# Last token group of an encoder layer: residual copied to the output, scaled tiles added to it by stores of GpSimd

## The reference, cut to what matters

```python
u = rms_norm(h, norm_pre)
p = u @ w_in                      # attention and linear-attention inputs, gates
y_a = (attention(...) * silu(za)) @ w_branch_attn
y_g = (rms_norm(gla(...)) * silu(zg)) @ w_branch_gla
merged = sigmoid(ga + b) * y_a + sigmoid(gg + b) * y_g
h = h + rms_norm(merged @ w_out, norm_post)
```

## Time and profile before

| | us |
|---|---|
| median of 3 runs | 2850.39 |
| lowest, highest | 2848.67, 2850.72 |
| profiled execution, whole time | 2849.08 |
| its span, first to last instruction | 2847.3 |
| TensorE busy in the span | 2746.1 |
| VectorE busy | 2120.7 |
| ScalarE busy | 1205.7 |
| GpSimd busy | 78.7 |
| DMA, mean rate | 160 GB/s |

### The profile page before, as it was taken

One profiled execution on the slowest core, in us unless ns is written; L12 is line 12 of the kernel. 1 busy time (PEld: TensorE's weight loads), 2 busy tenths in 40 slices (PEclk: granted clock), 3 DMA queues, 4 the chain that ended last, 5 costly groups with the idle time before them and its releaser, 6 DMA issues. The chain is left out here.

```text
span 2847.3 us, 52025 instructions
## 1 busy us (share of the span) xinstructions
PE 2746.1 (96%) x20860; PEld 2603.7 (91%) x20860; DVE 2120.7 (74%) x3375; ACT 1205.7 (42%) x1972; POOL 78.7 (3%) x55
## 2 busy tenths in 40 slices
PE   7999999998999999999999999999899999999996
PEld 7999999998999999999777887878799999999996
DVE  7898777778787787777777777787576877655556
ACT  5343333445354333344555566565422322442331
POOL 0221000000000000000000000000000000000001
PEclk9999999999999999999999999999999999999998
DMA  4555333345344333344656565565534555555664
GB/s 152 164 185 177 122 128 127 122 132 209 100 141 142 123 128 128 120 133 133 193 164 187 171 190 177 165 191 167 194 133 170 212 198 198 170 173 184 184 195 138
DMA packets 234186, 456.95 MB, mean 160 GB/s; under 512 B 23904, under 2 KB 139744, under 8 KB 233072
## 3 DMA queue, kind: packets, MB, share of 16 engines
q1 hardware_dynamic: 233968, 453.91, 49.8%
HBM read 365.90 MB, written 88.47 MB: 160 GB/s over the span
## 5 line engine op out<-in xcount | busy, mean ns | idle before, releaser
L2164 PE MATMUL bank<-th,w_hi 128*128 128x272 f32 x2360 | 687.3, 291 | 8.7 <-DVE w_lo L1429 6.4
L2164 PE MATMUL bank<-tl,w_hi 128*128 128x272 f32 x2360 | 682.7, 289 | 0.0
L2164 PE MATMUL bank<-th,w_lo 128*128 128x272 f32 x2360 | 682.0, 289 | 0.0
L2164 PEld LDWEIGHTS bank<-th,w_hi 128*128 128x128 f32 x2360 | 445.2, 189 | 13.1 <-DVE w_lo L1429 8.0
L1416 DVE TENSOR_TENSOR w_lo<-w_raw,w_hi 128x1024 fp32r<-128x1024 f32 x224 | 273.8, 1223 | 239.2 <-ACT w_hi L989 238.8
L1004 ACT ACTIVATE w_hi<-w_more 128x1024 fp32r<-128x1024 f32 x236 | 250.3, 1061 | 469.7 <-DVE w_more L1448 247.8
L2164 PEld LDWEIGHTS bank<-tl,w_hi 128*128 128x128 f32 x2360 | 445.3, 189 | 1.0 <-issue 1.0
L2164 PEld LDWEIGHTS bank<-th,w_lo 128*128 128x128 f32 x2360 | 444.9, 189 | 0.0
L989 ACT ACTIVATE w_hi<-w_raw 128x1024 fp32r<-128x1024 f32 x224 | 236.8, 1057 | 365.9 <-PE bank L2476 228.0
L1429 DVE TENSOR_TENSOR w_lo<-w_more,w_hi 128x1024 fp32r<-128x1024 f32 x236 | 295.1, 1251 | 111.0 <-ACT w_hi L1004 108.8
L2142 PE MATMUL bank<-uh,w_hi 128*128 128x272 f32 x1024 | 317.0, 310 | 13.5 <-DVE w_lo L1416 8.6
(11 more groups left out here) (278 smaller groups left out, 5653.1 us busy)
## 6 DMA issues: line engine op xcount, KB each, us to landing
w_raw<-in_w_tiles SPq DMA_DIRECT2D x344, 512.0 KB, 4.1
w_more<-in_w_tiles SPq DMA_DIRECT2D x120, 512.0 KB, 3.6
p_scratch<-stage SPq DMA_DIRECT2D x44, 544.0 KB, 3.0
gl<-p_scratch SPq DMA_DIRECT2D x24, 512.0 KB, 5.7
w_pair<-in_w_tiles SPq DMA_DIRECT2D x9, 1024.0 KB, 8.7
gate_scratch<-stage SPq DMA_DIRECT2D x16, 544.0 KB, 3.0
gate_scratch<-stage SPq DMA_DIRECT2D x64, 136.0 KB, 4.2
gate_even<-gate_scratch SPq DMA_DIRECT2D x8, 1088.0 KB, 6.8
```

Source lines behind the costliest of these rows:

```text
L2164: ins = pe.matmul(out[:, 0:GAW], wt[:, k], ut[:, k], start=start and k == 0 and i == 0, stop=stop and k == HK - 1 and i == 2, skip_group_c ...
```

## The change

The residual of the last group is no longer loaded into `x_last`. In place of the first `load_last`, behind the first pair of group 1, SyncE issues one transfer that copies all 2048 rows of the last group's tokens from `xT` to `yT`, from DRAM to DRAM. The wait for the products of group 0 that stood ahead of the first load is gone, and so are the other three loads. In the tail VectorE only scales; its additions and those of GpSimd are gone. GpSimd waits for the copy, and then for each pair of scaled tiles, and issues a store of the pair with an accumulating operation: what is stored is added to what lies in `yT`. SyncE no longer issues the last stores and only waits for them.

```diff
--- before.py
+++ after.py
@@ -489,10 +489,9 @@
         s_sld = sem("state_loaded")
 
         s_g = [sem("gates_of_even_pairs_loaded"), sem("gates_of_odd_pairs_loaded")]
-        s_xl = sem("last_residual_loaded")
+        s_xl = sem("last_residual_copied")
         s_yl = sem("last_output_stored")
         s_sc2 = sem("last_output_scaled")
-        s_add = [sem("last_even_tiles_added"), sem("last_odd_tiles_added")]
         s_oev2 = sem("output_tiles_evacuated")
         s_ssz = sem("square_sums_cleared")
         s_sqo = sem("output_squares_summed")
@@ -955,24 +954,13 @@
                         next_w(PASS_OUT + g * KT + m, m)
                         store_y(g - 1, n, m, r)
 
-                def load_last(k):
-
-                    a, w = GRP[2]
-                    sp.dma_start(x_last[:, k:k + 4, 0:w], x_view[:, k:k + 4, a:a + w]).then_inc(s_xl, 16)
-
                 pair(0)
                 if g == 1:
-                    sp.wait_ge(s_mo, 2 * KT)
-                load_last(8 * (g - 1))
+                    a, w = GRP[2]
+                    sp.dma_start(yT[:, a:a + w], xT[:, a:a + w]).then_inc(s_xl, 16)
                 with sp.Fori(1, KT // 2 - 1) as i:
                     pair(i)
-                load_last(8 * (g - 1) + 4)
                 pair(KT // 2 - 1)
-            a, w = GRP[2]
-            for i in range(KT // 2):
-                for r in range(2):
-                    sp.wait_ge(s_add[r], i + 1)
-                sp.dma_start(yT.rearrange("(k p) t -> p k t", p=P)[:, 2 * i:2 * i + 2, a:a + w], out_sb[2][:, 2 * i:2 * i + 2, 0:w]).then_inc(s_yl, 16)
             sp.wait_ge(s_yl, 16 * KT // 2)
             sp.wait_ge(s_kv, 16 * 6)
             sp.wait_ge(s_sst, 32)
@@ -1401,12 +1389,12 @@
                 gla_roots(it, DEC if it == N_IT - 1 else P)
             for n in range(3):
                 roots(n + 2, 3)
-            w = GRP[2][1]
-            for k in range(1, KT, 2):
-                pool.wait_ge(s_sc2, k + 1)
-                if k == 1:
-                    pool.wait_ge(s_xl, 16 * KT // 4)
-                pool.tensor_tensor(out_sb[2][:, k, 0:w], out_sb[2][:, k, 0:w], x_last[:, k, 0:w], ALU.add).then_inc(s_add[1], 1)
+            a, w = GRP[2]
+            y_view = yT.rearrange("(k p) t -> p k t", p=P)
+            pool.wait_ge(s_xl, 16)
+            for k in range(0, KT, 2):
+                pool.wait_ge(s_sc2, k + 2)
+                pool.dma_start(y_view[:, k:k + 2, a:a + w], out_sb[2][:, k:k + 2, 0:w], accum_op=ALU.add).then_inc(s_yl, 16)
 
 
         @block.vector
@@ -2126,11 +2114,6 @@
             for k in range(KT):
                 dve.scalar_tensor_tensor(out=out_sb[2][:, k, 0:w], in0=out_sb[2][:, k, 0:w], scalar=norm_sb[:, 1, k:k + 1],
                                          in1=rso[:, 0:w], op0=ALU.mult, op1=ALU.mult).then_inc(s_sc2, 1)
-                if k % 2 == 0:
-                    dve.wait_ge(s_sc2, k + 1)
-                    if k == 0:
-                        dve.wait_ge(s_xl, 16 * KT // 4)
-                    dve.tensor_tensor(out_sb[2][:, k, 0:w], out_sb[2][:, k, 0:w], x_last[:, k, 0:w], ALU.add).then_inc(s_add[0], 1)
 
 
         @block.tensor
```

## The result

The changed kernel took 2859.93 us in the median of 7 runs (2856.66 to 2861.8), the kernel before 2848.67 us in the 7 runs beside them (2846.24 to 2850.72). The ratio is 1.0035, with a 95% interval of 1.0025 to 1.0045: slower by about 10 us, 0.35% (the two medians lie 11.3 us apart). The profiled execution's span grew from 2847.3 to 2858.2 us, by 10.9 us.

A forecast was written before the change was run, and what follows sets the result against it. TensorE, busy for 96% of the span, was taken to bound the kernel, another engine only behind its last product. Stall 7.1, clock 2.0, tail -1.2 gave +7.9 us: 2857.0, or 2858.3 on the median's scale; range 2847 to 2869.

The forecast's parts named there:

- All three terms: Sum over the output stage and tail: stall 7.1, clock 2.0, tail -1.2, together +7.9 us.
- The copy's stall: Near 2590 us: 2.225 MB more ahead of the weights take 7.9 us, less 0.76 left over; TensorE stalls 7.1 us.
- the right one of the three: Rates considered for the copy ahead of the weights: 335, 280 and 219 GB/s; 280 was taken.
- The slow end: Bound for the copy near 2590 us: 219 GB/s for the whole copy, 10.9 us more, a stall of 10.1.
- The clock: Behind the pause near 2590 us: TensorE's granted clock falls, costing 2.0 us, with 0 and 2.4 as ends.
- The tail: Behind the last roots: additions leave, adding stores with bytes counted twice set the time; 1.2 us less, bounds -10.1 to +8.8.
- The later loads at 0: Output stage: the three later residual loads and the wait for the first products leave SyncE's queue, giving 0.
- A: Tail: adding stores run near the plain ones' rate, gaining about 8 us against the stall; 2851.5 us; chance 0.24.
- B: Tail: adding stores hardly overlap, eight of some 3.6 us one after the other, +8.8 us; 2868.3 us; chance 0.18.
- C: Near 2590 us: weights don't wait for the copy, late by less than 0.76 us; 2842.4 us with an 8 us tail gain; chance 0.12.

The follow-up runs named there:

- one load: The kernel before with its whole residual loaded into SBUF by one transfer of 2896 KB at the place of the first quarter; ratio 1.003 (1.0019 to 1.0041).

## Why the prediction was right

The forecast was 2858.3 us, and 2859.93 were measured. That these lie only 1.6 us apart is in part luck: the sum was +7.9 us, the spans differ by 10.9 and the medians by 11.3, and the kernel before was 1.7 us faster in the runs beside the changed kernel than in those that the forecast was put on. The mechanism was right in its main part, the stall and the clock. All three terms were too small: by 0.8, 0.4 and 1.7 us.

**The copy's stall: right in mechanism and place, 0.8 us too small.** The extra bytes were to delay the weights by 7.9 us and did so by 8.6; 0.76 us were to be left over, and 8.62 - 7.94 = 0.68 were. The rate of 280 GB/s was the right one of the three for the wrong reason: it was taken from residual loads that did not fill the engines, and the one large load runs at 384 to 392 GB/s. Over the 8.6 us of delay the 2.225 MB come to 258 GB/s. The slow end, from the small cache outputs, was nearer in kind, since they too go from DRAM to DRAM. That SyncE would be held for 4.42 us by its own next issue was not foreseen; whether it cost anything was not tried apart. The trace speaks against it: the weights' first issue was over at 2585.25, and the copy ahead of them landed only at 2594.8.

**The clock: right, 0.4 us too small.** 2.0 us were taken, 2.4 measured, as at the pause of the earlier trace rows. From the first product at 2598.95 TensorE worked at 0.50 for 4.7 us, which loses 2.35.

**The tail: the sign was wrong, by 1.7 us.** A gain of 1.2 us was forecast, a loss of 0.5 was measured, beyond even the 0 that the range took as this term's upper end. Counting the bytes twice came out right: 16.2 us were predicted for the eight transfers, and the engines were busy from 2840.0 to about 2856.7, 16.7 us; the receipt took 1.5 us for 1.4. The mis-sized term is the way of the first store. From the first pair's scaling to the first bytes the sum had 1.2 us of issue; the pair was ready at 2836.61 + 1.1 = 2837.7 and the bytes moved at 2840.0, 2.3 us later. That makes 1.1 of the 1.7 us. GpSimd's issue itself was well placed at 1.2 (1.25); but it began only at 2838.37, 0.7 us behind the ready pair. The Trainium skill, Collectives: The Full Stack (The bandwidth ceiling), says of the adding step of a collective that it needs two source reads and so runs at half the rate of a copy. The traces don't show the reads, but the rate agrees: 189 GB/s against 345 for the plain store, a factor of 1.8 for its 2.

**The later loads at 0: right, as far as the noise lets one see.** With the copy out of the weights' way the kernel is at 1.0004 of the one before, tail included.

**The rivals.** A fell with the windows of the tail: the DMA engines are full at 189 GB/s. B fell as well: the issues overlap with the transfers, and the stores flow without gaps. C named a condition that holds when the copy has a queue of its own (the pause is 2.22 us there), and not in the one that the weights stand in; even there the weights are late by more than the 0.76 us left over, so it would not have been faster.

## What to carry to other kernels

A transfer that nobody waits for still has a place in a queue: ask whose data stand behind it, and how many bytes their lead is worth (here 0.741 MB used up nearly all of it, and 1.483 MB were too many). Cut it, or issue it where the queue has nothing left to bring; the same copy cost 10 us behind the first pair and nothing behind the last weights. And work that is moved from engines into transfers is not gone: an adding store took 1.8 times as long as a plain one, so the tail changed its bound and kept its length. A split over both made it 16.8 us long, where all additions on VectorE gave 20.3.

## What the runs showed of the hardware

A longer pause of TensorE did not cost more clock. By ScalarE's steps, less the pause, the cost was:

| pause of TensorE, us | kernel | cost behind it, us | TensorE at work at 0.50, us |
|---|---|---|---|
| 1.78 | copy in halves, second | 0.3 | none |
| 2.22 | copy by ScalarE | 1.8 | 3.4 |
| 2.77 | copy in halves, first | 1.8 | 3.4 |
| 3.15 | copy by GpSimd | 3.0 | 6.2 |
| 5.42 | one load | 2.8 | 5.5 |
| 7.94 | the change | 2.4 | 4.7 |

The last column is read from windows of 0.5 us. The lower clock lasted longest in the change, for 10 us in all. But in the last three rows it fell while TensorE still stood, in the two above them only when it was at work again; and the cost is about half of the time for which TensorE worked at 0.50. So a stall of some 2 us can cost nearly twice its length. The length alone does not decide whether the clock falls. Two pauses of the kernel before, and the windows behind each:

```profile
699.45 0.39 PE L2164 MATMUL bank<-th,w_hi 128*128 128x272 f32 x1 [2.38 <-DVE w_lo L1429]
2055.37 0.39 PE L2142 MATMUL bank<-uh,w_hi 128*128 128x272 f32 x1 [2.07 <-DVE w_lo L1416]
```

```profile
700.00:705.00 5.00, 2.73 (x22) 2.51 (x20) 4.89 (x5) 2.57 (x5) 0.00 (x0) 1.00 0.16 68
2055.00:2057.00 2.00, 1.63 (x10) 1.63 (x11) 0.66 (x2) 1.30 (x2) 0.00 (x0) 0.78 1.08 388
```

The longer of the two left the clock at full, the shorter one did not.

The large copy from DRAM to DRAM in rows of 1448 bytes ran at 269 to 302 GB/s in the changed kernel, and a load of the same rows into SBUF at 384 to 392, both with full DMA engines; they landed in 15.7 and 13.1 us. VectorE's addition to one tile takes 0.54 us alone and 1.16 beside GpSimd's addition, but not beside GpSimd's issue of a transfer (two in 0.98 us).
